# Four of a decoder step's cached key chunks turned inside the prompt's attention

## The reference

```
q, k, v, qi, ki, wi, u = rms_norm(x) @ w_in          # 2048 -> 4688 columns
group A: sparse attention, 8 query heads, 2 KV heads, head_dim 128, rotary
         an indexer picks the top-k keys for each query (k = 128 prompt, 256 sampled);
         softmax(q.k * scale) over the picked keys, then times v
         prompt : keys are the 512 prompt tokens
         sampled: keys are 16 pages x 128 tokens per sequence, out of a paged cache
                  (cache_k, cache_v: page, 128 tokens, 2 KV heads, 128), and the 4 new tokens
group B: GLU, causal depthwise conv (31 taps), LayerNorm, swish
h = x + concat(A, B) @ w_out
y = rms_norm(h + (silu(n2 @ w_gate) * (n2 @ w_up)) @ w_down)
```

## Time and profile before

| | |
|---|---|
| median of 3 runs | 2526.94 us (2517.93 to 2528.32) |
| the profiled execution's own time | 2520.81 us |
| its span in the trace | 2519.2 us |
| PE busy | 98% of the span |
| DVE, ACT, POOL busy | 47%, 33%, 15% |
| mean granted PE clock | 0.997 |

### The profile page before, as it was taken

The page is one execution under the profiler, slowest core; times in us unless marked ns, Lnnn a source line. Parts: engine busy times, 40 slices in busy tenths (PEclk is TensorE's granted clock), DMA queues, the critical chain, the costliest instruction groups (busy, mean ns, idle before and its releaser), DMA issues.

```text
span 2519.2 us, 49839 instructions
## 1 busy us (share of the span) xinstructions
PE 2468.1 (98%) x19410; PEld 2389.0 (95%) x19412; DVE 1186.3 (47%) x1796; ACT 834.7 (33%) x1091; POOL 383.2 (15%) x430
## 2 busy tenths in 40 slices
PE   7999999999989999999999999999999999999998
PEld 6968999996679999999999999999999999999998
DVE  6688989887433352333333332433233333333354
ACT  6153344326322243333223333223333222222233
POOL 2334899623610000000000000000000000000000
PEclk9999999999999999999999999999999999999999
DMA  7414233315864443232233222233322223232232
GB/s 247 122 38 115 73 83 84 88 43 177 277 194 108 119 109 92 83 92 65 87 108 89 86 85 72 86 99 92 92 83 81 75 85 108 86 88 84 68 91 95
DMA packets 424729, 255.07 MB, mean 101 GB/s; under 512 B 19980, under 2 KB 413444, under 8 KB 423969
## 3 DMA queue, kind: packets, MB, share of 16 engines
q1 hardware_dynamic: 412864, 224.91, 31.0%
q0 software_dynamic: 11792, 29.23, 3.6%
HBM read 243.66 MB, written 11.27 MB: 101 GB/s over the span
## 4 chain that ended last, share of the span: by engine, by line
PE 86%; issue 4%; POOL 3%; DVE 3%; ACT 2%; DMA 1%; SPq 0%; POOLq 0%; DVEq 0%; ACTq 0%
PE ps L1566 80%; POOL y L577 3%; PE ps L1829 1%; PE ps L1659 1%; PE ps L1803 1%; PE ps L1849 1%; ACT tap L762 1%; PE ps L1785 1%; DMA xN<-in_x_prompt 1%; PE ps L1878 0%; DMA stN<-in_state_conv 0%; POOL tapS L585 0%; PE ps L1942 0%; PE ps L1749 0%; PE ps L1742 0%
## 5 line engine op out<-in xcount | busy, mean ns | idle before, releaser
L987 DVE TENSOR_TENSOR wlo<-raw,whi 128x1024 fp32r<-128x1024 f32 (+1 forms) x366 | 447.9, 1225 | 1098.1 <-ACT whi L636 1084.7
L1566 PE MATMUL ps<-xhi,whi 128*128 128x272 f32 (+1 forms) x4512 | 935.4, 288 | 8.8 <-DVE xlo L995 2.8
L1566 PE MATMUL ps<-xhi,wlo 128*128 128x272 f32 (+1 forms) x4512 | 934.1, 288 | 0.0
L1566 PE MATMUL ps<-xlo,whi 128*128 128x272 f32 (+1 forms) x4512 | 930.3, 288 | 0.0
L636 ACT CAST whi<-raw 128x1024 fp32r<-128x1024 f32 (+1 forms) x410 | 429.0, 1048 | 1167.6 <-PE ps L1566 1090.2
L1566 PEld LDWEIGHTS ps<-xhi,whi 128*128 128x128 f32 (+1 forms) x4512 | 708.5, 188 | 12.5 <-issue 3.9
L1566 PEld LDWEIGHTS ps<-xlo,whi 128*128 128x128 f32 (+1 forms) x4512 | 708.4, 188 | 0.0
L1566 PEld LDWEIGHTS ps<-xhi,wlo 128*128 128x128 f32 (+1 forms) x4512 | 703.7, 189 | 0.0
L1566 PE MATMUL ps<-hidh,whi 128*128 128x272 f32 x1408 | 291.4, 288 | 0.0
L1566 PE MATMUL ps<-hidl,whi 128*128 128x272 f32 x1408 | 291.2, 288 | 0.0
L1566 PE MATMUL ps<-hidh,wlo 128*128 128x272 f32 x1408 | 291.1, 288 | 0.0
(11 more groups left out here) (314 smaller groups left out, 1551.4 us busy)
## 6 DMA issues: line engine op xcount, KB each, us to landing
raw<-in_w_gate SPq DMA_DIRECT2D x88, 512.0 KB, 3.7
raw<-in_w_up SPq DMA_DIRECT2D x88, 512.0 KB, 3.8
raw<-in_w_in SPq DMA_DIRECT2D x72, 512.0 KB, 3.8
raw<-in_w_down SPq DMA_DIRECT2D x64, 384.0 KB, 3.4
raw<-in_w_down SPq DMA_DIRECT2D x64, 320.0 KB, 3.2
raw<-in_w_out SPq DMA_DIRECT2D x32, 512.0 KB, 5.3
ring_pages<-in_cache_k SPq DMA_DIRECT2D x40, 128.0 KB, 3.6
ring_pages<-in_cache_k POOLq DMA_DIRECT2D x40, 128.0 KB, 3.5
```

The source lines that it names most:

```text
L987: ve.tensor_tensor(wlo[:, u.slot, :, 0:cols], raw[:, u.slot, :, 0:cols], whi[:, u.slot, :, 0:cols].bitcast(F32), ALU.subtract).then_inc(s_ ...
L1566: ins = te.matmul(ps[0:cols, 2 * slot + half, 0:HALF], w[:, u.slot, t, 0:cols], x[:, k0 + t, HALF * half:HALF * half + HALF], start=(hf == ...
```

## The change

PE turns chunks q = 0 to 3 inside the prompt's loop: in each of the iterations x = 14 to 21 it turns one half-chunk (one KV head, four transposes) at the end of the iteration, `early_half(x - 14)`. ACT copies head 0 of chunk q in its iteration x = 15 + 2q, between the exponential and the copy of the transposed weights; DVE copies head 1 in its iteration x = 16 + 2q, between the negated maximum and the normalisation. All eight halves use PSUM bank 5, so each half waits for the copy of the half before it. The scores of the prompt give that bank up and take turns over three (0, 1, 4).

The slots of chunks 0 to 3 are refilled with chunks 18 to 21 as soon as each was turned, and the last two slots, which wait for all scores, get chunks 22 and 23. From 24 on chunk n again waits for n - 20, except that chunks 60 and 61 wait for 42 and 43 (40 and 41 before).

```
+EARLY = 4
+EARLY_AT = 14
...
+        def chunk_before(n):
+            if n < OSLOTS + 2:
+                return None
+            if n < OSLOTS + 2 + EARLY:
+                return n - OSLOTS - 2
+            if n < SLOTS + EARLY:
+                return None
+            return n - SLOTS if n < 60 else n - 18
...
         def half_bank(q, kv):
-            return 5 + (2 * q + kv) % 3
+            return 5 if q < EARLY else 5 + (2 * q + kv) % 3
...
-                if n >= SLOTS:
-                    eng.wait_ge(s_chunk, 2 * ((n if n < 62 else n + 2) - SLOTS + 1))
+                if chunk_before(n) is not None:
+                    eng.wait_ge(s_chunk, 2 * (chunk_before(n) + 1))
...
-                elif n == OSLOTS + 2:
+                elif n == OSLOTS + 2 + EARLY:
                     eng.wait_ge(s_s, 32)
...                                                              # ACT, after the exponential of x
+                if EARLY_AT < x <= EARLY_AT + 2 * EARLY and (x - EARLY_AT) % 2:
+                    q = (x - EARLY_AT) // 2
+                    act.wait_ge(s_mix, CT)
+                    act.wait_ge(s_chunk, 2 * q + 1)
+                    nc.scalar.copy(turned_keys(q, 0), ps[:, half_bank(q, 0), :]).then_inc(s_kca, 1)
...                                                              # DVE, after the negated maximum of x
+                if EARLY_AT < x <= EARLY_AT + 2 * EARLY and (x - EARLY_AT) % 2 == 0:
+                    q = (x - EARLY_AT) // 2 - 1
+                    dve.wait_ge(s_chunk, 2 * q + 2)
+                    ve.tensor_copy(turned_keys(q, 1), ps[:, half_bank(q, 1), :]).then_inc(s_kcd, 1)
...                                                              # PE
+            def early_half(m):
+                q, kv = divmod(m, 2)
+                if m >= 1:
+                    pe.wait_ge((s_kcd, s_kca)[kv], q + kv)
+                keys_half(q, kv)
...
-                    bank = (0, 1, 4, 5)[x % 4]
-                    if x >= 4:
-                        pe.wait_ge(s_p, x - 3)
+                    bank = (0, 1, 4)[x % 3]
+                    if x >= 3:
+                        pe.wait_ge(s_p, x - 2)
...                                                              # PE, end of iteration x
+                if EARLY_AT <= x < EARLY_AT + 2 * EARLY:
+                    early_half(x - EARLY_AT)
```

More of the change, by code:

```diff
@@ L376, in block_head, with slot_number @@
             return x % 16 // 4, 4 * (x // 16) + x % 4
+        def chunk_before(n):
[6 more added lines that the diff above has]
+            return n - SLOTS if n < 60 else n - 18
+        def slot_number(n):
+            if chunk_before(n) is not None:
+                return slot_number(chunk_before(n))
+            return n if n < OSLOTS + 2 else n - EARLY
         def page_slot(n):
-            s = n % SLOTS if n < 62 else n - 58
+            s = slot_number(n)
             if s >= OSLOTS:
@@ L817, in _ @@
                         act.wait_ge(s_pt, x - 2)
-                    nc.scalar.activation(pP[:, x % 3, 0:w], ps[:, (0, 1, 4, 5)[x % 4], 0:w], ACT.Exp,
+                    nc.scalar.activation(pP[:, x % 3, 0:w], ps[:, (0, 1, 4)[x % 3], 0:w], ACT.Exp,
                                          bias=stat[:, 24 + x % 4:25 + x % 4], scale=ASCALE,
                                          accum_out=stat[:, 28 + x % 4:29 + x % 4]).then_inc(s_p, 1)
+                if EARLY_AT < x <= EARLY_AT + 2 * EARLY and (x - EARLY_AT) % 2:
[3 more added lines that the diff above has]
+                    nc.scalar.copy(turned_keys(q, 0), ps[:, half_bank(q, 0), :]).then_inc(s_kca, 1)
                 if x == 1:
@@ L854, in _ @@
             for g in range(2):
-                for q in range(16 * g, 16 * g + 16):
+                for q in range(max(16 * g, EARLY), 16 * g + 16):
                     act.wait_ge(s_chunk, 32 * g + 2 * q + 1)
@@ L1378, in _ @@
                         dve.wait_ge(s_p, x - 3)
-                    ve.reduce_max(stat[:, 36 + x % 4:37 + x % 4], ps[:, (0, 1, 4, 5)[x % 4], 0:w], AX.X
+                    ve.reduce_max(stat[:, 36 + x % 4:37 + x % 4], ps[:, (0, 1, 4)[x % 3], 0:w], AX.X
                                   ).then_inc(s_nm2, 1)
@@ L1768, in _, with pages_landed, keys_half, keys @@
             tile(P_V, 1)
+            def pages_landed(n):
+                pe.wait_ge(s_pg[n // 2 % PAIRS], 32 * SPP * (n // SLOTS + 1))
+                pe.wait_ge(s_pgp[n // 2 % PAIRS], 32 * (4 - SPP) * (n // SLOTS + 1))
+            def keys_half(q, kv):
+                n = 32 * (q // 16) + q % 16
+                if n % 2 == 0 and kv == 0:
+                    pages_landed(n)
+                for k in range(4):
+                    ins = te.transpose(ps[:, half_bank(q, kv), P * k:P * k + P],
+                                       page_slot(n)[:, k, P * kv:P * kv + P], ident[:, :])
+                ins.then_inc(s_chunk, 1)
+            def keys(q):
+                for kv in range(NKV):
+                    if kv == 0 and q >= 2:
+                        pe.wait_ge(s_kcd, q - 1)
+                    if kv == 1 and q >= 1:
+                        pe.wait_ge(s_kca, q)
+                    keys_half(q, kv)
[3 more added lines that the diff above has]
+                    pe.wait_ge((s_kcd, s_kca)[kv], q + kv)
+                keys_half(q, kv)
             pe.wait_ge(s_bias, 1)
@@ L1811, in _ @@
             pe.wait_ge(s_ol, 8)
[L1813 to L1831, removed]
             for g in range(2):
@@ L1843, in _ @@
                     q0 = 16 * g + 4 * c
-                    for q in range(q0, q0 + 4):
+                    for q in range(max(q0, EARLY), q0 + 4):
                         keys(q)
```

## The result

| | before | changed |
|---|---|---|
| median of 20 runs each | 2522.58 us (2517.14 to 2528.32) | 2528.53 us (2525.32 to 2535.36) |
| ratio, 95% interval | | 1.0026 (1.0017 to 1.0034) |
| profiled execution: span | 2519.2 us | 2524.9 us |
| PE, from the score product of x = 14 to the first output product | 594.21 to 716.03: 121.8 us | 592.75 to 723.53: 130.8 us |
| of it the loop, up to the first bias product of the sampled attention | to 631.90: 37.7 us | to 644.01: 51.3 us |

The changed kernel is slower by 0.26% by the ratio, 6.6 us, with an interval of 4.3 to 8.6 us (the two medians differ by 6.0). The forecast was +10. In the traces the two attention stages take 9.0 us more; the rest of the two executions differs by 3.3 us the other way.

What follows compares the result with a forecast made beforehand. The prediction took PE, busy 98% of the span, as the bound. Its terms, -3.9 + 0 + 3.6 + 3.9 + 6.1 - 0.9 + 1.2, gave +10.0 us on 2523.9, so 2534 us, range 2525 to 2541.

Steps and rivals of the forecast that it cites:

- the case that I gave most weight: Whole kernel: landing wait and single bank cost far more than the removed stretch gives; net delay 7 to 12.5 us, chance 0.57.
- the rival in which the loads give it back: End of sampled attention: fewer chunks left to load remove PE's 3.9 us of last-value waits; net +6 us, chance 0.14.
- the signs named beforehand: Trace after: page wait 2.3 to 5.2 us, copy waits some 6, prompt's end 13 to 15 later, last-value waits about unchanged.
- What leaves the sampled stage: Sampled attention up to the first values: the first 32 transposes go, -3.86 us.
- The earlier refill: Loads of chunks 20 onward: later loads keep their distance to PE's releases, so 0; 3.9 us at most if wrong.
- The landing: PE after iteration 14: waits for the pages of chunks 0 and 1, 2.3 to 5.2 us, taken as +3.6 us.
- The eight halves: PE's prompt loop: the same 32 transposes now stand there, +3.86 us unless they fill idle time.
- idle time filled: Prompt loop: new waits cover PE's idle time in iterations 16, 20 and 21, less a longer wait at 23; -0.9 us.
- The one bank: Iterations 15 to 21: each half waits for the copy of the half before out of bank 5; +6.1 us.
- The clock: Behind the landing wait: PE's clock may fall to 1.2 GHz; +1.2 us, bounds -1.7 and +1.7.
- The level: Whole kernel's time: 2534 us, from 2523.9 for the kernel before plus the sum of +10.0.
- The halves fit into the loop: Prompt loop: copies come before PE needs the bank and pages have landed; -1.9 to -5.8 us, chance 0.05.

Runs made afterwards that it cites:

- e3: The changed kernel, but POOL reads the first 32 page numbers before waiting for the key rows; ratio 1.0023 to before, loop 46.2 us against 51.3.
- e5: The changed kernel with the slot order and refill of before, early turning kept; ratio 1.0044 to before, stretch 130.3 us against 130.8.
- e8: The kernel before, with PE waiting for the pages of chunks 0 and 1 at the end of iteration 14; ratio 1.0014, loop 40.1 us against 37.7.
- e10: The same kernel as e5 run again, beside e11; ratio 1.0035 to before, stretch 128.8 us.
- e6: The kernel before with its scores over three banks, nothing turned early; ratio 0.9996, loop 37.7 us as before.
- e2: The changed kernel with scores over two banks and the halves over two, 5 and 4; ratio 1.0014 to before, loop 46.2 us against 51.3.
- e4: The changed kernel with the changes of e2 and e3 together; ratio 0.9991 to before, loop 41.2 us, stretch 120.6 us against 121.8 before.
- e11: The changed kernel run a third time, unchanged, beside e10; ratio 1.0031 to before, stretch 129.3 us.
- e7: The changed kernel run again, unchanged; ratio 1.0027 to before, stretch 130.4 us.
- e9: The kernel before, with the first four chunks turned right behind the loop, ahead of the wait for the last low halves; ratio 0.9999, stretch 119.4 us against 121.8.

## Why the prediction came out as it did

The direction, the mechanism and the range were right: "within 0.5%", slower, 2528.5 in 2525 to 2541. The likeliest value was 3.4 us too high as a difference, 10.0 against 6.6, and 1.4 above the upper end of the interval. The number alone would not have singled out the case that I gave most weight: +6.6 us lies below its band of 7 to 12.5, and nearer to the rival in which the loads give it back (+6). It is the traces and e3, e5, e8 and e10 that decide between them. Of the signs named beforehand the landing wait, the waits for the copies (4.5 us by the view, little over the 4 that would have refuted it) and the later end of the loop (13.6 us, counted from x = 14) came; the waits for the last values shrank instead of staying. Point by point:

- **What leaves the sampled stage**, -3.86. From the stage's first product to the first values it is 25.95 us after and 30.16 before: -4.2, and -4.6 up to the first output product. 0.3 us of the surplus is the first group's products, which start with all copies long made: 1.85 us (644.36 to 646.21) against 2.13; all traces with early turning have it (25.9 to 26.0). The last 0.4 lies behind the first values, where the three traces of the changed kernel differ by 0.2 among themselves, and before, e6 and e8 by 0.5.
- **The earlier refill**, 0. Right, and by the reason given: in all thirteen traces POOL had stood idle for 3.0 to 3.8 us when PE released chunk 36, and the last product with values came 47.8 to 49.6 us after, whatever the kernel. e3, e5 and e10 show it by experiment. "The 3.9 us of waits stay" was wrong in detail: they fell to 2.5. They are what PE has left over while it waits for the transfers: PE lost time at 680 to 684 us at the slow clock and waited that much less later, while the distance from the release to the last product stayed. The other traces bear that out. In seven a stretch of slow clock sets in within 10 us behind the release of chunk 36, and the waits are 2.3 to 2.9 us; in six it does not, and they are 3.4 to 4.9 (4.9 in e2, 4.2 in e4), whether the kernel turns early or not. That the distance itself varies by 1.8 us stays unexplained.
- **The landing**, +3.6. Measured 3.58, by the view. It is no constant, though: 2.9 to 3.5 in five other traces, 2.2 in e8, since PE and POOL do not come to it with one distance. Over the three traces of the changed kernel it is 3.2, and 3.4 with the 0.16. The early draw of PE in the first trace (its x = 14 was 1.5 us ahead of before) made it long.
- **The eight halves**, +3.86, and **idle time filled**, -0.9. e4 has both without the waits: loop +3.5 with 3.9 added, so 0.3 was filled, net, less than I took. In the changed kernel the new waits cover idle time too, and there it is more than I took (the sum, below).
- **The one bank**, +6.1. Six waits, 4.5 us by the view of the waits and about 5.5 by the starts. The term is right for x = 17 to 21 within 0.1 us each. x = 15 was short (0.56 by the view) because PE's own work behind its scores ran at the slow clock and came later to the bank: in e3, e10 and e11, where the clock stayed at 1.00, the wait is 0.93, and all waits of the term sum to 5.9 by the starts. e2 took away 5.1, as some of the idle time that these waits cover comes back without them.
- **The clock**, +1.2. From the first half to the second it is 5.3 us in the first trace and 5.5 in e7, where the clock fell, and 4.0 in e11: 1.3 and 1.5 us. The clock fell behind the landing wait in four traces (changed, e2, e5, e7) and not in e8, e10 and e11. The Trainium skill ("TensorE: Matmul & The Clock Gate", section "HAM oscillation - how this bites in real kernels") has it fall behind each wait for a transfer that is long enough. These traces do not bear out that the length decides: waits of 2.93, 3.23, 3.53 and 3.58 us were followed by the fall, those of 3.05 and 3.17 us were not. The gaps at 656 and 696 us, by which I had weighed it, were no waits for transfers, and both are equally long:

```profile
658.31 2.08 PE L1864 MATMUL ps<-ident,pS 128*128 128x128 f32 x12 [1.95 <-ACT pS L865]
698.55 1.99 PE L1864 MATMUL ps<-ident,pS 128*128 128x128 f32 x12 [1.95 <-ACT pS L865]
```

- The sum of the loop was 13.9 (3.6 + 3.9 + 6.1 - 0.9 + 1.2). The three traces of the changed kernel gave 13.6, 13.1 and 11.8, mean 12.8. By the starts the mean is made up of 3.4 for the landing, 3.9 for the halves, 5.9 for the one bank and 0.9 for the clock (1.3, 1.5 and 0, from half to half, so with the shorter wait at x = 15 taken off), less 1.25 of idle time filled. The last is what is left over of the sum, and comes out as 1.2 to 1.3 in each of the three and in e3, e5 and e10 as well. So each term but the halves was mis-sized by 0.2 to 0.4 us, all towards too long a loop. With -4.5 instead of -3.9 for the stage the traces give +9.0, +8.5 and +7.5, and the ratios +6.6, +6.8 and +7.8. What lies between the two sets, about 1.3 us, is within the intervals; it stays open whether it is more than chance.
- The level, 2534, was also 1.3 us high, as I took 2523.9 for the kernel before and twenty runs gave 2522.58.

The rivals: the loads do not give it back (e3, e5, e8, e10). The halves fit into the loop only with a second bank and early pages, and then the gain is within the noise (e4: 1.3 us by the stretch). What the change means to use, idle time in the loop, was hardly there: without the new waits only some 0.3 of 3.9 us found room (e4), and the refill feeds loads that were not late.

## What to carry to other kernels

Work that is moved into a loop of three engines costs its own time, less the idle time there, and for a single shared buffer the whole chain of the iteration as well: sum, for each iteration, when the buffer comes free and when the engine comes back to it. An earlier load helps only if the loads that somebody waits for follow it by time; where they follow by releases of the very engine that waits, look for the release, not at the queue. And a gap that already exists (the 1.5 us behind the loop) is a better place for moved work than a loop that is nearly full: by the traces e9 gains 1.6 us there, which the times (0.9999) can't confirm.

## What the runs showed of the hardware that was not expected

**The start falls into two groups.** The score product of x = 0 came at 567.9 to 569.9 us in seven traces and at 573.7 to 576.0 in six, nothing between, for changed and unchanged kernels alike (568.6 for before, 576.0 for e6, whose code up to there is the same). The split is in the first 40 us. Windows of e6, then of before, 32 to 40 us:

```profile
32.00:36.00 4.00, 0.66 (x4) 0.42 (x4) 1.52 (x4) 3.97 (x9) 0.77 (x1) 0.99 0.83 258
36.00:40.00 4.00, 3.33 (x15) 3.33 (x16) 3.88 (x7) 3.60 (x7) 0.00 (x0) 0.50 0.68 223
```

```profile
32.00:36.00 4.00, 2.83 (x23) 2.83 (x24) 3.65 (x6) 3.60 (x8) 0.00 (x0) 1.00 1.10 363
36.00:40.00 4.00, 4.00 (x35) 3.77 (x33) 3.86 (x11) 2.15 (x5) 0.72 (x1) 1.00 1.04 293
```

In e4, e5 and e6 PE is busy for only 0.7 of the first 4 of these 8 us; in the other three of the late group the gap is less whole. But from 38 to 40 us the granted clock is 0.50 in all six of the late group, and 1.00 in all seven of the early one. What starts it is not settled. The 5 to 6 us between the groups and the 4.9 us by which the rest of the execution differs (1799.8 to 1804.7 us after the first output product) add up to about the spread of the times, 2517 to 2528 for before; that they are its whole cause is not shown.

**Like gaps, other clocks.** Waits of 2.93 to 3.58 us were followed by the 1.2 GHz level in four traces, waits of 3.05 and 3.17 us were not in two; and of two gaps of 1.95 us in the kernel before, one was and one was not. Such a stretch cost nothing where the engine waits for transfers anyway: from the release of chunk 36 to the last product with values it was 48.5 us with it (changed) and without it (before).
